# Forgetting attention in a two-block transformer kernel: decay bias from running sums kept as rows, added by 8-partition products

## The reference, cut to what matters

```python
f_logit = proj[..., o:o + FOX_HEADS] + b_f
cum = jnp.cumsum(jax.nn.log_sigmoid(f_logit), axis=1)
...
sf = jnp.einsum('bqhd,bkhd->bhqk', qf, fk) * (FOX_HEAD_DIM ** -0.5)
sf = sf + cum[q, h] - cum[k, h]            # written here with indices
pf = jax.nn.softmax(jnp.where(causal, sf, NEG_2), axis=-1)
of = jnp.einsum('bhqk,bkhd->bqhd', pf, fv)
```

## Time and profile before

| | us |
|---|---|
| median of 3 runs | 924.67 |
| lowest and highest | 924.28, 924.98 |
| the profiled execution | 925.52 |
| its span, first to last instruction | 923.7 |
| TensorE busy | 871.4 (94% of the span) |
| VectorE busy | 595.8 (65%) |
| ScalarE busy | 464.2 (50%) |
| GpSimd busy | 78.4 (8%) |

### The profile page before, as it was taken

How to read it: one execution, slowest core, us unless ns; L and a number is a source line. 1 busy time by engine, 2 the same in 40 slices (tenths; PEclk the granted TensorE clock), 3 DMA queues, 4 the chain that set the end, 5 groups by cost and what they waited for, 6 DMA issues and landing times.

```text
span 923.7 us, 15564 instructions
## 1 busy us (share of the span) xinstructions
PE 871.4 (94%) x6246; PEld 806.8 (87%) x6246; DVE 595.8 (65%) x765; ACT 464.2 (50%) x649; POOL 78.4 (8%) x78
## 2 busy tenths in 40 slices
PE   3999897999999999999999999989998999999997
PEld 3999796999889899798999999879985799999995
DVE  4348757534877768688777677776545676666554
ACT  5356773235855623566456455664545454333332
POOL 0024652100000032000000000000000000000000
PEclk9999898999999999999999999999999999999999
DMA  8452343143333345635655555353322545555541
GB/s 322 173 183 92 138 137 131 52 150 114 138 137 138 104 176 184 226 133 176 223 178 186 182 182 189 132 182 106 124 92 69 182 160 184 187 189 194 193 144 46
DMA packets 21736, 143.83 MB, mean 156 GB/s; under 512 B 3008, under 2 KB 3012, under 8 KB 5168
## 3 DMA queue, kind: packets, MB, share of 16 engines
q1 hardware_dynamic: 19872, 138.30, 42.3%
q0 software_dynamic: 1808, 4.73, 1.5%
HBM read 141.96 MB, written 1.84 MB: 156 GB/s over the span
## 4 chain that ended last, share of the span: by engine, by line
PE 82%; DVE 8%; ACT 5%; issue 3%; DMA 1%; POOL 1%; SPq 0%; ACTq 0%; DVEq 0%; POOLq 0%
PE pj L472 16%; PE pj L474 14%; PE pj L475 14%; PE pa L877 6%; PE pa L878 6%; PE pa L879 6%; DVE w_lo L1563 2%; PE pj L477 2%; PE pj L476 2%; DVE area L1576 2%; PE pa L511 2%; ACT w_hi L1116 1%; PE pj L573 1%; DVE area L1579 1%; PE po L607 1%
## 5 line engine op out<-in xcount | busy, mean ns | idle before, releaser
L1563 DVE TENSOR_TENSOR w_lo<-w_raw,w_hi 128x2048 fp32r<-128x2048 f32 x128 | 300.0, 2346 | 78.1 <-ACT w_hi L1116 78.1
L472 PE MATMUL pj<-a_hi,w_hi 128*128 128x256 f32 x1184 | 340.3, 287 | 9.7 <-DVE w_lo L1563 9.1
L474 PE MATMUL pj<-a_lo,w_hi 128*128 128x256 f32 x1184 | 337.2, 285 | 0.0
L475 PE MATMUL pj<-a_hi,w_lo 128*128 128x256 f32 x1184 | 337.0, 285 | 0.0
L1116 ACT ACTIVATE w_hi<-w_raw 128x2048 fp32r<-128x2048 f32 x128 | 243.8, 1907 | 69.9 <-PE pa L879 41.5
L472 PEld LDWEIGHTS pj<-a_hi,w_hi 128*128 128x128 f32 x1184 | 229.4, 194 | 15.3 <-issue 14.3
L474 PEld LDWEIGHTS pj<-a_lo,w_hi 128*128 128x128 f32 x1184 | 229.5, 194 | 0.8
L475 PEld LDWEIGHTS pj<-a_hi,w_lo 128*128 128x128 f32 x1184 | 229.3, 194 | 0.0
L877 PE MATMUL pa<-w_hi,a_hi 128*128 128x512 f32 x280 | 109.5, 391 | 4.2 <-issue 4.2
L878 PE MATMUL pa<-w_lo,a_hi 128*128 128x512 f32 x280 | 109.2, 390 | 0.0
L879 PE MATMUL pa<-w_hi,a_lo 128*128 128x512 f32 x280 | 109.0, 389 | 0.0
(11 more groups left out here) (248 smaller groups left out, 1041.5 us busy)
## 6 DMA issues: line engine op xcount, KB each, us to landing
w_raw<-stream SPq DMA_DIRECT2D x128, 1024.0 KB, 4.8
area<-gains POOLq DMA_DIRECT2D x4, 512.0 KB, 4.2
cst<-consts SPq DMA_DIRECT2D x1, 1093.0 KB, 13.9
x_tok<-x_in SPq DMA_DIRECT2D x2, 512.0 KB, 4.5
area<-cmpw POOLq DMA_DIRECT2D x1, 1024.0 KB, 5.5
out<-x_tok SPq DMA_DIRECT2D x4, 256.0 KB, 2.0
t_wide<-t_rows POOLq DMA_DIRECT2D x1, 768.0 KB, 13.6
prm<-params SPq DMA_DIRECT2D x1, 562.5 KB, 10.2
```

The source lines that it names most:

```text
L472: pe.matmul(out_, a[0], a[1], start=first, stop=False)
L474: pe.matmul(out_, wh, al, start=False, stop=False)
L475: return pe.matmul(out_, wl, ah, start=False, stop=last)
L1563: dve.tensor_tensor(w_lo[:, slot, :], w_raw[:, slot, :], w_hi[:, slot, :].bitcast(F32), ALU.subtract)\
```

## The change

The bias no longer comes from triangles. Since `cum[q, h]` is one value for a softmax row, it is left out, and only `-cum[k, h]` is added, as a row of keys.

- VectorE writes the log forget values 16 times over (`lf8`: for each half of the tokens 16 x 8 columns), in two instructions instead of one.
- TensorE gets `f_sums`, once: `lf8` is the stationary operand of two float32 products with `le_ones` and `le`, so that all 128 partitions of `po` hold running sums, partition 8a+b those of head b. It stands after unit fq 0.
- ScalarE copies them with the sign turned to `ncum` (128x256), between `exps(10)` and the copy of `d_turn(2)`. Partitions 0 to 7 and 64 to 71 are used later.
- `f_scores` has four products for each head: q with k as before, and twice a one-hot column of `ident` on 8 partitions, repeated 128 times by a stride of zero, with 8 rows of `ncum`. They stand on partitions 0:8 for one head and 64:72 for the other. The two heads' products now follow each other, kind by kind.
- GpSimd's four triangle products and the buffers `lfle` are gone.

```diff
@@
+        ncum = V(56, T)
+        lf8 = V(54, 2, 16, 8)
@@ GpSimd
-            for j in range(4):
-                if j == 0:
-                    gp.wait_ge(S("lf_ready"), 1)
-                elif j >= 2:
-                    gp.wait_ge(S("S_written"), USE["S"].index(f"f{j - 2}") + 1)
-                gp.tensor_tensor(lfle[j % 2], le.unsqueeze(1).unsqueeze(1).to_broadcast([P, 2, 2, P]),
-                                 lf[:, :, 2 * j:2 * j + 2].unsqueeze(3).to_broadcast([P, 2, 2, P]),
-                                 ALU.mult).then_inc(S("lfle_ready"), 1)
@@ TensorE, f_scores(j)
-                pe.wait_ge(S("lfle_ready"), j + 1)
+                await_read(pe, "O", "fcum")
+                o_ = [ps[:, hb, :] for hb in range(2)]
+                q = [slice(hb * 64, hb * 64 + 64) for hb in range(2)]
+                hot = [ident[64 * hb:64 * hb + 8, 64 * hb + 2 * j + hb:64 * hb + 2 * j + hb + 1].to_broadcast([8, P])
+                       for hb in range(2)]
+                row = [ncum[64 * hb:64 * hb + 8, :] for hb in range(2)]
                 for hb in range(2):
-                    q = slice(hb * 64, hb * 64 + 64)
-                    o_ = ps[:, hb, :]
-                    ll = lfle[j % 2]
-                    pe.matmul(o_[:, 0:128], fq[q, j, 0:P], fk[q, j, 0:P], start=True, stop=False)
-                    pe.matmul(o_[:, 0:128], ll[:, 0, hb, :], gt, start=False, stop=True)
-                    pe.matmul(o_[:, 128:384], fq[q, j, P:T], fk[q, j, 0:T], start=True, stop=False)
-                    pe.matmul(o_[:, 128:384], ll[:, 1, hb, :], ones_gt, start=False, stop=True)
-                    mm = pe.matmul(o_[:, 128:256], lf[:, 0, 2 * j + hb:2 * j + hb + 1].to_broadcast([P, P]), gt,
-                                   start=False, stop=True, skip_group_check=True)
+                    pe.matmul(o_[hb][:, 0:128], fq[q[hb], j, 0:P], fk[q[hb], j, 0:P], start=True, stop=False)
+                for hb in range(2):
+                    pe.matmul(o_[hb][:, 0:128], hot[hb], row[hb][:, 0:P], start=False, stop=True)
+                for hb in range(2):
+                    pe.matmul(o_[hb][:, 128:384], fq[q[hb], j, P:T], fk[q[hb], j, 0:T], start=True, stop=False)
+                for hb in range(2):
+                    mm = pe.matmul(o_[hb][:, 128:384], hot[hb], row[hb], start=False, stop=True)
                 written(mm, "S")
+
+            def f_sums():
+
+                claim(pe, "O", "fcum")
+                pe.wait_ge(S("lf_ready"), 2)
+                heads = [lf8[:, tb, :, :].rearrange("p a b -> p (a b)") for tb in range(2)]
+                pe.matmul(po[:, 0:T], heads[0], le_ones, start=True, stop=False, skip_group_check=True)
+                written(pe.matmul(po[:, P:T], heads[1], le, start=False, stop=True, skip_group_check=True), "O")
@@ TensorE's order
             run_unit(("fq", 0))
+            f_sums()
             d_turn(2)
@@ ScalarE's order
             exps(10, sm2, pr2)
+            await_psum(act, "O", "fcum")
+            read(act.activation(ncum, po[:, 0:T], ACT.Copy, scale=-1.0), "O")
             d_turned(2)
@@ VectorE
-            stt(lf, fl, 0.0, lf_e, ALU.min, ALU.subtract).then_inc(S("lf_ready"), 1)
+            for tb in range(2):
+                stt(lf8[:, tb], fl[:, tb].unsqueeze(1).to_broadcast([P, 16, 8]), 0.0,
+                    lf_e[:, tb].unsqueeze(1).to_broadcast([P, 16, 8]), ALU.min, ALU.subtract)\
+                    .then_inc(S("lf_ready"), 1)
```

More of the change, by code:

```diff
@@ L237, in program @@
         od, odsq, dg8, odn = V(50, 4, T), V(0, 4, T), V(4, 8, P), V(0, 4, T)
-        lfle = [V(54, 2, 2, P), V(56, 2, 2, P)]
+        ncum = V(56, T)
+        lf8 = V(54, 2, 16, 8)
         t5_sb, narrow = V(20, 384), V(12, T)
@@ L261, in program @@
         lamv, lm = small(8), small(4)
-        lf, lf_e, fl = small(2, 8), small(2, 8), small(2, 8)
+        lf_e, fl = small(2, 8), small(2, 8)
         ods = small(8)
@@ L286, in program @@
             + [f"n{j}" for j in range(4)] + ["rbc1", "rbc2",
-               "flog", "flog_tok", "d0", "d1", "odn", "f0", "f1", "f2", "f3", "rbc3"]
+               "flog", "flog_tok", "d0", "fcum", "d1", "odn", "f0", "f1", "f2", "f3", "rbc3"]
         USE = {"S": S_USE, "T": T_USE, "O": O_USE}
```

## The result

The changed kernel takes 917.87 us (median of 6 runs, 916.59 to 918.31), against 925.39 us of the kernel before in the same comparison (6 runs, 924.28 to 925.97): a ratio of 0.9918, interval 0.9905 to 0.9931. It is faster by 7.5 us. Its profiled execution took 917.97 us with a span of 916.2 us, 7.5 less than before.

What follows compares the result with a forecast made beforehand. TensorE, busy for 94% of the span, was taken as the bound. Profiled execution: 925.52 - 9.36 (score blocks) + 0.40 (`f_sums`) = 916.6 us; the same 8.96 off the 924.67 median gave 915.7 us, range 913.0 to 918.6.

Steps and rivals of the forecast that it cites:

- B: Score blocks: the 8-partition pairs run one after the other, +2.6 us, 918.3 us; chance 0.14.
- D: Sparser score blocks bring one stretch of mostly 1.2 GHz clock to 701 to 712: 3.4 us lost, 919.1 us; chance 0.07.
- A: Likeliest case: both heads overlap in every step of a score block, 2.10 us a block, 915.7 us; chance 0.62.
- Score blocks: Four blocks on TensorE: each falls from 4.44 to 2.10 us, steps 0.41, 0.42, 0.63, 0.63; saving 9.36 us.
- `f_sums`, +0.40 us: Two added TensorE products before `d_turn(2)`: 0.66 us, of which 0.26 lie in an existing gap and 0.40 remain.
- ScalarE and VectorE at nothing: ScalarE's sign-turning copy and VectorE's two log steps fit where waits already stand: 0 us each.
- The saving survives the softmax chain: Behind the score blocks: the softmax work starts from each block's end and moves with it, so the saving counts whole.
- The clock: TensorE's granted clock: no loss from it in the sum; a half-speed stretch was considered only as a rival.
- Rival F: Score blocks: each of 16 records loaded and drained by itself, 5.8 us a block, 930.5 us; chance 0.03.

Runs made afterwards that it cites:

- the filled kernel: The changed kernel plus seven filler products in the three gaps where TensorE waits behind the last score block: 916.14 us, ratio 0.9903.
- the order undone: The changed kernel with each score block's eight products reordered, all four of the first head, then all four of the second: 931.38 us.
- both heads on the same partitions: The changed kernel with both heads' one-hot products reading partitions 0 to 7: 921.83 us.
- the shifted kernel: The changed kernel with five filler products, 2.15 us in all, ahead of `f_scores(0)`: 920.06 us.

## Why the prediction was right, and where not

Forecast were 915.7 us, 913.0 to 918.6; the median is 917.87. Direction and range held. The time is 2.2 us above the forecast; of that, 1.4 are gain that did not come (8.96 forecast, 7.52 measured in the same comparison), and 0.7 are the kernel before, which took 925.39 us there and 924.67 in the runs that the forecast started from. That the range held owes something to luck: 917.87 is nearer to the 918.3 of B and the 919.1 of D than to A, and the range reached so far because of B, which did not come.

- **Score blocks, 2.10 us each.** Right to the hundredth, step by step, and for the reason given: 0.2 us for each change of kind and full overlap of the two halves. Other orders and operands of these products gave 4.16, 2.75, 1.71 and 1.51 us where 4.16, 2.76, 1.7 and 1.5 had been worked out from the earlier trace rows. One reading was off: what the longer old blocks had beyond 4.44 us was not the follower's and did not stay. The last one went from 4.62 to 2.10, and the four together save 9.63 us (18.03 to 8.40) instead of 9.36. By these rows its old end paid for a change of kind too, to the 128*64 product behind it; the new block's last step of 0.63 holds such a change already, whatever follows.
- **`f_sums`, +0.40 us.** Its products start at 644.71 and the transposes at 645.36. Against the earlier trace rows, with the marks 0.79 us apart, the transposes are 0.32 us later: 645.36 - (645.83 - 0.79). The gap hid half of it.
- **ScalarE and VectorE at nothing.** Right. The copy took 0.38 us and `d_turned(2)` follows it at once; the two log steps took 0.49 us ahead of a split that still waited 1.31 us for ScalarE.
- **The saving survives the softmax chain.** Right. VectorE's scaling ends at 666.53 + 1.01 = 667.54, and `f_turn(0)` starts at 667.94 behind its projection, no idle time before it; the distance was 0.22 us and is 0.40. The gain was not handed on to a wait: up to `f_turn(3)` it is 9.2 us.
- **The clock.** This term was put at nothing in the sum, and it is what is missing. Rival D, with a chance of 0.07, named the place, and the stretch came in both profiles of the changed kernel; that the sparser blocks bring it, as D had it, is not shown. The sum of A holds only with the clock up (9.15 us less in the filled kernel, 8.96 worked out). As a price 3.4 us was too high: TensorE was busy for 6.05 of the 6.8 us, the wait for the output projection shrank from 1.29 to 0.75 us, and the cost was 2.3 us. The only row behind the small chance was the 1.00 in 701 to 712, where TensorE was busy for 6.97 of 11.00 us: gaps that had got by once were taken for gaps that get by.
- **Rival F,** the slower one, had its mechanism wrong. One head after the other does become slower than before, by 6 us, but not by serial loads: its four blocks are 1.41 us shorter than the old ones (16.62 against 18.03), and the clock takes about 7.1 us (137.62 - 131.60 = 6.02, and 1.41 less 0.32 for the sums on top).

## What to carry to other kernels

Small products on TensorE cost by their neighbours: put those that use the same number of partitions together, one on each half, and give the odd ones as many partitions as their neighbours (with 64 instead of 8 a block took 1.51 us instead of 2.10). After shortening work ahead of idle time on TensorE, read the granted clock of the stretch behind it again, for a 1.00 before does not carry over; fillers in gaps of 1 to 3 us were worth 1.5 to 2.7 us of the stage here where the clock had been falling, and nothing that the median shows where the stretch was already short. Compare the distance of two marks around the changed stage, besides the total, and take more than one profile: the half-level stretches of one kernel are not the same in each execution.

## What was not expected of the hardware

TensorE without a single idle moment in the profile can get its clock halved. With blocks of 4.16 us of products on 64 and 8 partitions, one after the other, it was at 0.50 behind each of the first three; with 128 partitions instead of 8, in the same order, and blocks of 3.90 to 4.18 us, it stayed at 1.00 through all of them. The profile counts both as equally busy (40.00 of 40.00 us), so the busy share does not tell them apart. These are one profile each, but the others point the same way: of the seven profiles whose blocks have products on 8 partitions, three have half-level stretches behind blocks and away from any wait (the order undone, both heads on the same partitions, the shifted kernel); of the seven without such products, none has. Why it is three and not all seven stays open.
